# Final norm of all rows beside the last eight expert slots

## The reference, cut to what matters

```python
for e in range(N_EXPERTS):
    he = jax.nn.silu(h @ p['expert_w_gate'][e]) * (h @ p['expert_w_up'][e])
    y = y + gate[..., e:e + 1] * (he @ p['expert_w_down'][e])
x = x + y
return x * lax.rsqrt(jnp.mean(x * x, axis=-1) + NORM_EPS) * norm_final
```

## Time and profile before

| what | us |
|---|---|
| median of three runs | 1232.5 (1231.83 to 1233.97) |
| the profiled execution | 1233.92 |
| its span, first to last instruction | 1232.2 |
| PE busy in the span | 1162.6 (94%) |
| last matmul starts / SP's last store issued | 1198.34 (32 of them) / 1226.72 |

### The profile page before, as it was taken

One profiled execution on the slowest core, in us unless ns is written; L12 is line 12 of the kernel. 1 busy time (PEld: TensorE's weight loads), 2 busy tenths in 40 slices (PEclk: granted clock), 3 DMA queues, 4 the chain that ended last, 5 costly groups with the idle time before them and its releaser, 6 DMA issues. The chain is left out here.

```text
span 1232.2 us, 31435 instructions
## 1 busy us (share of the span) xinstructions
PE 1162.6 (94%) x12690; PEld 830.3 (67%) x12690; DVE 525.3 (43%) x1250; ACT 336.9 (27%) x785; POOL 567.2 (46%) x821
## 2 busy tenths in 40 slices
PE   7999999999999999999999999689999999999990
PEld 6788878756656677787754545367777777777760
DVE  5466986644394425645523113532222222222223
ACT  5002012352441244564433222201111111111114
POOL 7512221110750248788632021046666666666661
PEclk9999999999999999999999999899999999999995
DMA  7401120134104110000075214499999897998838
GB/s 214 103 1 36 36 69 18 36 103 117 48 19 95 51 21 17 23 16 17 20 240 186 82 69 137 131 357 374 317 373 341 256 373 238 290 374 254 274 51 298
DMA packets 142874, 187.12 MB, mean 152 GB/s; under 512 B 39464, under 2 KB 89247, under 8 KB 142778
## 3 DMA queue, kind: packets, MB, share of 16 engines
q1 hardware_dynamic: 126010, 164.87, 39.6%
q0 software_dynamic: 15936, 20.57, 8.0%
q10 hardware_dynamic: 832, 0.33, 0.1%
HBM read 156.41 MB, written 29.32 MB: 151 GB/s over the span
## 5 line engine op out<-in xcount | busy, mean ns | idle before, releaser
L526 PE MATMUL ps<-hT,w_in 128*128 128x352 f32 (+1 forms) x624 | 192.6, 464 | 1.8 <-ACT cb L816 1.2
L526 PEld LDWEIGHTS ps<-hT,w_in 128*128 128x128 f32 x624 | 116.4, 190 | 66.5 <-issue 4.1
L3129 POOL DMA_INDIRECT sum_rows<-slot_out,scatter_rows x76 | 121.9, 1604 | 38.9 <-POOL scatter_rows L3128 26.1
L3261 DVE TENSOR_TENSOR slot_T<-slot_raw_T,vecs 128x256 f32<-128x256 f32 x75 | 32.8, 438 | 209.4 <-PE ps L3174 208.2
L3174 PE MATMUL ps<-qkv,slot_T 128*32 128x256 f32 x1920 | 109.9, 379 | 3.7 <-DVE slot_T L3261 2.5
L3174 PEld LDWEIGHTS ps<-qkv,slot_T 128*32 128x32 f32 x1920 | 74.8, 110 | 32.9 <-DVE slot_T L3261 4.8
L3106 POOL DMA_INDIRECT gathered<-h_rows,gather_rows x79 | 83.5, 1057 | 19.3 <-issue 12.2
L3218 ACT ACTIVATE slot_silu<-ps 128x128 f32<-128x128 f32 x77 | 21.5, 279 | 223.7 <-PE ps L3174 221.5
L3174 PE MATMUL ps<-cb,slot_T 128*32 128x256 f32 x1408 | 80.6, 379 | 0.0
L3174 PEld LDWEIGHTS ps<-cb,slot_T 128*32 128x32 f32 x1408 | 55.4, 110 | 20.5
L3224 ACT ACTIVATE slot_out<-ps,slot_weights 128x256 f32<-128x256 f32 x76 | 36.1, 475 | 112.6 <-PE ps L3185 112.6
(11 more groups left out here) (765 smaller groups left out, 2369.7 us busy)
## 6 DMA issues: line engine op xcount, KB each, us to landing
qkv<-in_expert_w_gate SPq DMA_DIRECT2D x6, 2048.0 KB
qkv<-in_expert_w_up SPq DMA_DIRECT2D x6, 2048.0 KB
qkv<-in_expert_w_down SPq DMA_DIRECT2D x6, 2048.0 KB
cb<-in_expert_w_gate SPq DMA_DIRECT2D x5, 2048.0 KB
cb<-in_expert_w_up SPq DMA_DIRECT2D x5, 2048.0 KB
zg<-in_expert_w_down SPq DMA_DIRECT2D x5, 2048.0 KB
third_w_down<-in_expert_w_down SPq DMA_DIRECT2D x5, 2048.0 KB
w_in<-in_w_in SPq DMA_DIRECT2D x18, 512.0 KB, 5.1
```

What stands on the lines that cost most here:

```text
L526: last = pe.matmul(pbank(b)[:, c, 0:n], w[:, k, :], hT[:, k, c * CH:c * CH + n], start=(k == 0), stop=(k == KD - 1))
L3129: pool.indirect_dma_start(quarter_sums, bass.IndirectOffsetOnAxis(ap=sidx[:, r:r + 1], axis=0), y[r][:], None, compute_op=ALU.add).then_in ...
L3261: dve.tensor_tensor(xT[:], xr[:], bc(nf, 2, ROWS_SLOT), ALU.mult).then_inc(s.xT, 1)
```

## The change

The eight slots of the last two rounds (68 to 75 here, two of them empty) are no longer added to `sum_rows`. All loops run over the earlier slots only and the last eight are written out one by one (`i` = 0 to 7). As soon as the adds of the earlier slots have landed, SP loads all nine tiles of `sum_rows`, the sample tile first, into buffers of their own; they are squared on ACT, scaled and stored beside the last slots' work. The last eight slots' outputs go to two tiles `last_y` of 128 whole rows (a slot's 32 rows by four quarters, two quarters on ACT and two on DVE, all four on ACT for the last two slots). For each, POOL gathers the same rows of `sum_rows` (`sums`), the two are added (`add_sums`), normed as tiles 9 and 10, and written by indirect DMAs over what the nine tiles had stored. The reciprocal root is now POOL's power of -0.5 (`scale`), three instructions a tile, instead of ACT's Ln and Exp. DVE forms the row numbers of the last slots before its loop. The load of `norm_final` moves from the end to behind the third expert's weights. Tiles live also in the masks' buffer (one wide tile now), `slot_out`, `part[1]` and `last_y`, whose reuse waits for the stores of tiles 8, 0 and 1 (`f.os`, `f.o0`, `f.o1`).

```diff
+                step(dve.tensor_scalar, fours[:], incl[:, NE - 1:NE], 1.0 / RING, (RING - 1.0) / (2 * RING) - 2.0, ALU.mult, ALU.add)
                 step(dve.tensor_scalar, fours[:], fours[:], ROUND, None, ALU.add)
...
-                dve.tensor_scalar(route.first[:, NE + 3:NE + 4], fours[:], -ROUND, None, ALU.add)
+                for a, n in ((2, 1.0), (3, float(RING)), (4, 16.0)):
...
+        LATE = 2 * RING
...
+        last_y = [T.sb(f"last_out_{a}", P, D) for a in range(2)]
+        part = [T.sb(f"last_sums_{a}", P, D) for a in range(2)]
+        wrow = T.sb("norm_final_rows", P, D)
+        early = [T.sb(f"early_rows_{a}", P, D) for a in range(4)]
+        tile_of = [part[1][:], last_y[1][:], m.run[:], slot_out[:]] + [e[:] for e in early] + [last_y[0][c4[3]]]
...
+        mean, rstd = T.sb("row_mean_squares", P, TILES + 2), T.sb("row_scales", P, TILES + 2)
+        minus_half = T.sb("minus_half", P, 1)
...
+                load(2)
+                sp.dma_start(wrow[:], A["norm_final"].partition_broadcast(P)).then_inc(f.w, 16)
+                for j in range(3, NE):
                     load(j)
-                landed = [sp.value_load(route.first[0:1, NE + 4 + r:NE + 5 + r], min_val=32 * NE // RING, max_val=16 * SLOTS // RING) for r in range(RING)]
-                sp.wait_ge(s.gu, bound(sp, NE - 2))
-                sp.dma_start(wrow, A["norm_final"].partition_broadcast(P)).then_inc(f.w, 16)
+                landed = early_landed(sp)
                 for r in range(RING):
-                    sp.wait_ge(out_y[r], landed[r])
-                for t in range(TILES):
-                    sp.dma_start(x[t][0:n[t]], sum_rows[t * P:t * P + n[t], :]).then_inc(x_in[t], 16)
-                for t in range(TILES):
-                    sp.wait_ge(f.y, t + 1)
+                    sp.wait_ge(out_y[r], landed)
+                for t in [NT] + list(range(NT)):
+                    sp.dma_start(tile_of[t], sum_rows[t * P:t * P + (P if t < NT else NS), :]).then_inc(x_in[t], 16)
+                for n, t in enumerate([NT] + list(range(NT))):
+                    sp.wait_ge(f.y, n + 1)
                     dst = O["y_prompt"][0, t * P:t * P + P, :] if t < NT else O["y_sample"].rearrange("b t d -> (b t) d")
-                    sp.dma_start(dst, x[t][0:n[t]]).then_inc(f.out, 16)
-                sp.wait_ge(f.out, 16 * TILES)
+                    sp.dma_start(dst, tile_of[t]).then_inc({NT: f.os, 0: f.o0, 1: f.o1}.get(t, f.out), 16)
+                sp.wait_ge(f.os, 16)
+                sp.wait_ge(f.o0, 16)
+                sp.wait_ge(f.o1, 16)
+                sp.wait_ge(f.out, 16 * (NT - 2))
+                sp.wait_ge(f.late, 16 * 4)
...
+                def last_rows(q, r, loads, landed=None):
+                    pool.wait_ge(in_ring[r], 16 * loads)
+                    pool.wait_ge(s.xTp, q + 1)
+                    pool.wait_ge(s.xg, q)
+                    if landed is not None:
+                        for x in range(RING):
+                            pool.wait_ge(out_y[x], 16 * landed)
+                    pool.tensor_copy(idx[:, r:r + 1], route.token[:, ds(q + RING, 1)])
+                    pool.tensor_copy(xg[:], ring[r][:]).then_inc(s.xg, 1)
...
+                def sums(a):
+                    pool.indirect_dma_start(part[a][:], None, sum_rows,
+                                            bass.IndirectOffsetOnAxis(ap=row_of[:, a:a + 1], axis=0)).then_inc(part_in[a], 16)
+                def scale(t):
+                    pool.wait_ge(f.sq, nth[t])
+                    pool.tensor_scalar(mean[:, t:t + 1], mean[:, t:t + 1], NORM_EPS, None, ALU.add)
+                    pool.drain()
+                    pool.tensor_tensor(rstd[:, t:t + 1], mean[:, t:t + 1], minus_half[:], ALU.pow).then_inc(f.rstd, 1)
+                def add_sums(a, q):
+                    pool.wait_ge(f.half, RING * a + RING)
+                    pool.wait_ge(s.acc, q + 2)
+                    pool.wait_ge(part_in[a], 16)
+                    pool.tensor_tensor(last_y[a][:], last_y[a][:], part[a][:], ALU.add).then_inc(f.sum, 1)
+                def last_out(a):
+                    pool.indirect_dma_start(O["y_prompt"][0], bass.IndirectOffsetOnAxis(ap=row_of[:, a:a + 1], axis=0), last_y[a][:], None,
+                                            bounds_check=SEQ - 1, oob_is_err=False).then_inc(f.late, 16)
+                def last_sample_out(a):
+                    pool.indirect_dma_start(O["y_sample"].rearrange("b t d -> (b t) d"), bass.IndirectOffsetOnAxis(ap=sample_of[:, a:a + 1], axis=0),
+                                            last_y[a][:], None, bounds_check=NS - 1, oob_is_err=False).then_inc(f.late, 16)
...
+                pool.memset(minus_half[:], -0.5)
...
-                m = more_rounds(pool)
+                n = early_rounds(pool)
+                first = early_slots(pool)
...
-                with pool.Fori(1, m) as i:
...
+                next_rows(first + RING, 0, n + 2, RING + 2 * first)
+                pool.wait_ge(f.idx, 1)
+                last_rows(first + RING + 1, 1, n + 2, landed=n)
+                sums(0)
+                scale(NT)
+                scale(0)
+                scale(1)
+                last_rows(first + RING + 2, 2, n + 2)
+                scale(2)
+                scale(3)
+                scale(4)
+                last_rows(first + RING + 3, 3, n + 2)
+                pool.wait_ge(f.o0, 16)
+                sums(1)
+                scale(5)
+                scale(6)
+                add_sums(0, first + RING - 1)
+                scale(7)
+                scale(TILES)
+                pool.wait_ge(f.norm, 1)
+                pool.wait_ge(f.os, 16)
+                last_sample_out(0)
+                pool.wait_ge(f.o0, 16)
+                pool.wait_ge(f.o1, 16)
+                pool.wait_ge(f.out, 16 * (NT - 2))
+                last_out(0)
+                scale(TILES + 1)
+                pool.wait_ge(f.norm, 2)
+                last_out(1)
+                last_sample_out(1)
+                pool.wait_ge(f.late, 16 * 4)
...
-                pe.sem_inc(s.gu, RING + 2)
-                pe.sem_inc(s.down, RING + 2)
+                pe.sem_inc(s.gu, RING)
+                pe.sem_inc(s.down, RING)
...
+                def silu(q, first=False, hidden=False):
                     act.wait_ge(s.gu, q + 1)
+                    if hidden:
+                        act.wait_ge(s.he, q)
...
+                def last_rows(i, q):
+                    act.wait_ge(s.down, q + 1)
+                    if i == 3:
+                        act.wait_ge(f.os, 16)
+                    if i == 4:
+                        act.wait_ge(f.o1, 16)
+                    for c in range(quarters_on_act(i)):
+                        act.activation(last_y[i // RING][c4[i % RING], c * QD:c * QD + QD], y_bank[c4[c], 0:QD], ACT.Copy,
+                                       scale=route.weight[c4[c], ds(q, 1)])
+                    act.drain()
+                    if i < BOTH:
+                        act.wait_ge(f.half, i + 1)
+                    act.sem_inc(s.acc, 1)
+                def mean_square(t):
+                    rows, p = rows_of(t)
+                    if t < TILES:
+                        act.wait_ge(x_in[t], 16)
+                    else:
+                        act.wait_ge(f.sum, t - TILES + 1)
+                    if nth[t] > 1:
+                        act.wait_ge(f.sq, nth[t] - 1)
+                    act.activation(wide[p], rows, ACT.Square, scale=D ** -0.5, accum_out=mean[p, t:t + 1]).then_inc(f.sq, 1)
...
-                with act.Fori(1, rounds(act)) as i:
+                with act.Fori(1, early_rounds(act)) as i:
...
-                act.preload_act_table_set(LNEXP)
...
+                first = early_slots(act)
+                ahead = {2: (1,), 3: (4,), 4: (7,)}
+                behind = {1: (NT, 0), 2: (2, 3), 3: (5, 6), 4: (TILES,), 7: (TILES + 1,)}
+                for i in range(LATE):
+                    if i < LATE - 1:
+                        silu(first + i + 1, hidden=True)
+                    for t in ahead.get(i, ()):
+                        mean_square(t)
+                    last_rows(i, first + i)
+                    for t in behind.get(i, ()):
+                        mean_square(t)
...
-                def hidden(q, first=False):
...
+                def hidden_T(q, first=False):
...
+                def last_rows(i, q):
+                    dve.wait_ge(s.down, q + 1)
+                    if i == 3:
+                        dve.wait_ge(f.os, 16)
+                    if i == 4:
+                        dve.wait_ge(f.o1, 16)
+                    for c in range(2, 4):
+                        last = dve.tensor_scalar(last_y[i // RING][c4[i % RING], c * QD:c * QD + QD], y_bank[c4[c], 0:QD],
+                                                 route.weight[c4[c], ds(q, 1)], None, ALU.mult)
+                    last.then_inc(f.half, 1)
+                def add_sums(a, q):
```

(76 more changed lines are left out.)

61 lines of the change are left out of this document (25 added, 36 removed).

## The result

The changed kernel takes **1242.45 us** (1241.02 to 1244.77), the kernel before 1232.2 beside it: a ratio of **1.0081 [1.0067, 1.0095]**. It is slower by some 10 us, where 1224.8 was forecast, and lies above the range.

The account below looks back on a forecast made before the run. PE's 5.2 us a slot and a serial tail of 31.9 us were taken as the bound. Span saved 9.8 less start 2.1 is 7.7; 1232.5 less 7.7 gives 1224.8 us, range 1218.5 to 1231.5.

Parts of the forecast that it names:

- The step that failed: Each `scale` on POOL: two small operations and gaps, about 0.7 us; 1.25 behind an indirect DMA.
- 1.7, 1.1 and 1.9: Three holds of PE: before gate-up of slots 72 and 73 and before `down(73)`, 4.7 us in all.
- holds of 1 to 3 us are priced at the full clock: PE's work behind its late-slot holds was taken to run at the full clock, 2.4 GHz.
- the start forecast: Small operations ahead of DVE's loop delay PE at slot 2: 2.1 us, within bounds of nothing to 3.2.
- The tail: After PE's end: last norms, copies, sum and two indirect stores, from PE's end at 1205.0 to span end at 1222.4.
- A quarter: Copy of 32x256 of a late slot's output, on ACT or DVE: 0.36 us each, assuming successive copies overlap.
- the rule that the prediction weighed: Two-input DVE instructions and POOL's SBUF reads block each other: scales up to 1.2 us later, first two holds 2.4, 1227.2.
- Rival 1: DVE and ACT find `scale` done in time, so the holds of 4.7 us vanish: 1220.1; chance 20%.
- Rival 2: Landing takes 8 us in a shared queue, PE held 2 us more, end 4.9 later: 1229.7; chance 12%.
- Rival 3: POOL's power in the eleven scales is dear; at 2 us more each the time is 1236.5; chance 10%.
- Rival 4: One code-fetch pause of some 6 us in POOL's first `scale` moves PE and the end by 6.0: 1230.8; 5%.
- Wrong if `scale` takes over 1 us: Named sign in the new trace: a POOL `scale` above 1 us would show the forecast wrong.

Follow-up runs that it names:

- experiment 1: Changed kernel with the drain between each scale's two small operations replaced by a wait on the first one's own semaphore; 1234.81 us, ratio 1.0023.
- experiment 4: experiment 1 plus one POOL drain right behind the last early scale, before its wait for the stores; 1231.53 us, ratio 0.9983.
- experiment 6: experiment 1 reordered: scales ahead of the gathers of sums, norms later, ACT's square of tile 9 one slot later; 1232.13 us, ratio 0.9994.
- experiment 9: experiment 7 with tile 9's sum on DVE, drain earlier, square and norm 4 moved, row-number operations behind DVE's early loop; 1223.82 us, ratio 0.9921.
- experiment 2: Changed kernel, drain kept, with the power of -0.5 in each scale made a multiplication; 1241.41 us, ratio 1.0075.
- experiment 5: experiment 1 plus a plain wait for the first gather of sums to land, where the first drain stood; one execution, 1244.33 us.
- experiment 7: experiment 6 plus the one early drain of experiment 4; 1228.71 us, ratio 0.9966.

## Why the prediction was wrong

**The step that failed** is a price. `scale` on POOL was taken as "two small operations of 0.23 and gaps of 0.1, about 0.7", and behind an indirect DMA as 1.25. One of these gaps is `pool.drain()`. In nine of the eleven scales it was 0.15 to 0.32, near the price; behind the two gathers it was 8.67 and 3.30. The row that was chosen as nearest, a copy of 0.77 behind an indirect DMA, is of an instruction that does not wait for DMAs, and could not show it. The trace of before did have one row of the right kind, the drain of 2.52 at the end of POOL's last block; it was not read. (The one of 2.80 at 799.6 is not: all but 0.07 of it is operations ahead of it.) It also had a late landing: the last adding DMA, behind the nine loads, took 8.5 us where 3.7 was taken from the earlier trace rows.

**What it did.** In the changed kernel holds of 10.6, 0.2 and 7.6 stand where 1.7, 1.1 and 1.9 were forecast: 13.6 us more. The clock adds 3.9, where "holds of 1 to 3 us are priced at the full clock": for holds of this length that no longer held, and even behind the 4.33 of experiment 1 the last down took 3.33, though behind its two holds of 2.01 the gate-up took 3.66. That makes 17.5 of the 17.7 us by which PE's end missed (1207.1 with the start forecast, 1224.8 measured). The tail was sized well: 17.4 forecast, 18.2 measured.

**Without the drain** (experiment 1) the steps can be read one by one. Holds 8.35 instead of 4.7: 3.65 more. Cold last down: 1.4. The start: gate-up of slot 0 to that of slot 2 is 11.61, against 10.24 before, 1.4 instead of 2.1: 0.7 less. Tail 22.65 instead of 17.4: 5.25, of which 5.0 are the drain that every block ends with, which the forecast did not price. 1224.8 and 9.6 are 1234.4; 1234.81 was measured. The forecast of 7.7 us for the change was therefore out of reach in this order of work even without the drain; experiment 4, with both drain costs covered, gains 0.17% (some 2 us).

**Why the holds were 3.65 longer.** A quarter on DVE took 0.49 and on ACT 0.46, not 0.36 (two on each side a slot): copies that follow each other did not overlap, two on DVE took 0.98. And a small operation of POOL that falls under a norm takes as long as the norm, as here in the changed kernel:

```profile
1200.54 1.28 DVE L3401 SCALAR_TENSOR_TENSOR last_sums<-last_sums,row_scales,norm_final_rows 128x1024 f32<-128x1024 f32 x1
1200.59 1.31 POOL L3171 TENSOR_SCALAR row_mean_squares<-row_mean_squares 128x1 f32<-128x1 f32 x1
```

It took 0.22 alone and 1.31 here. This is the rule that the prediction weighed (the Trainium skill, SBUF — State Buffer, section Who interferes with whom); the traces agree that one waits for the other, in both directions (the norm of 3.74 above). Which of the two waits the records do not tell: the norm's starts 0.27 us ahead of the sum's, and still the norm was the slow one. The rule bore out, and the sum should have included it. The order is the other part: moving scales, norms and a square gave back 3.6 us (experiment 6). How the 3.65 divide among quarters, ports and order no run shows.

**The rivals.** Rival 1 (late work hides) did not happen in the changed kernel; experiment 9 comes nearest to its 1220.1, at 1223.8, still above its own range (1218.5 to 1222), after work on the holds that it named and on the drain and the start, which it did not. Rival 2 (landings of 8 us) was right on a number, the gather took 8.2, but nothing in its mechanism needed that early; it was the drain that made POOL wait for it. The stores did not land late: in the changed kernel SP's of whole tiles took 2.6 us, and POOL's four indirect ones 2.3 to 3.3 where 3.8 was taken. Rival 3 (the power is dear) named the right place, `scale`, and the right sign, with the wrong instruction: the power costs 0.57 where 0.23 was taken, and leaving it out changed nothing measurable (experiment 2). Rival 4 (POOL fetches code once, about 6 us): no run shows it. In experiment 1 the first power starts 0.09 after the operation ahead and takes 0.59. The 6 us that the Trainium skill, GPSIMD Engine Reference, section Instruction dispatch, gives for the first call to a freshly loaded kernel did not show here.

**The signs that were named** came out so: first of nine loads forecast at 1177 to 1180, issued at 1180.0; PE's gap before slot 72 with the sample tile's norm on DVE just ahead, the place right, 10.6 for 1.7; before `down(73)` 7.6 for 3; PE's end at 1224.8 for 1207; tail without waiting for a load, right; PE's wait at slot 2 "near 3" was 0.6 behind a gate-up on a cold clock in the changed kernel's profile and 1.7 in experiment 1. "Wrong if `scale` takes over 1 us" was the sign that counted.

## What to carry to other kernels

A drain is a wait and is priced as one. On POOL it waits for the indirect DMAs that POOL has issued, up to their landing behind whatever loads are under way, and the first drain after a long stretch of them cost several us more. Soon after another drain, with nothing outstanding, it left a gap of 0.15 us; between two dependent operations a semaphore of the engine's own orders as well and cost 0.1 whatever was outstanding. A drain's record in the profile also holds the operations ahead of it, so read the gap behind the last of them. Where a block ends right behind POOL's last stores, one drain placed earlier, where POOL idles, takes some 5 us off the end (4.9 in experiment 4).

When work is moved beside a loop that bounds the kernel, the mean room of each engine says nothing: write the order on each in-order engine for one period, and keep what waits (indirect DMAs, norms that need a scale) behind what the bounding engine is about to need.

## What the runs showed of the hardware that was not expected

- POOL's drain held the engine 8.6 us behind a 0.5 MB gather and 3.2 behind the second, where it ended 0.1 us after the landing; 5.01 at the block's end with all DMAs landed and none drained since the stage began; 0.22 to 0.38 with an earlier drain in the stage; 0.05 with no indirect DMA since the last.
- An indirect gather of 128 rows landed 8.2 us after issue behind the nine loads (experiment 5), where the adding DMA of the earlier trace rows took 3.7.
- A norm and a POOL operation slow each other: 0.22 to 1.31 for one column, 1.28 to 3.74 for the norm beside 128x1024 (experiment 7).
- The granted clock was down to 0.50 by 1196 where PE had stopped at 1190, and still 0.50 from 1198 to 1202.
